# Rest parts of the projection weights on GpSimd instead of VectorE, in a decoder layer on one core

## The reference

```
h = rms_norm(x, attn_norm)
proj = h @ w_in                         # 1024 x 3072: mq mk mv dq dk dv
q, k = rope(rms_norm(q)), rope(rms_norm(k))
moba = softmax(causal(q k^T / 8)) v
diff = rms_norm((softmax(q1 k1^T / 8) - lam * softmax(q2 k2^T / 8)) v) * (1 - lambda_init)
x = x + concat(moba, diff) @ w_out
h = rms_norm(x, ffn_norm)
x = x + (silu(h @ w_gate) * (h @ w_up)) @ w_down      # hidden width 2816
```

## Time and profile before

| | before |
|---|---|
| median of 3 runs | 684.35 us (684.1 to 685.02) |
| profiled execution, span from first to last instruction | 685.7 us |
| TensorE matmul busy | 654.8 us (95%) |
| TensorE weight load busy | 533.4 us (78%) |
| VectorE busy | 366.3 us (53%) |
| ScalarE busy | 247.9 us (36%) |
| GpSimd busy | 79.3 us (12%) |
| chain that ended last, by engine | PE 77%; DVE 14%; issue 4%; ACT 2%; DMA 1% |

### The profile page before, as it was taken

One profiled execution on the slowest core, in us unless ns is written; L12 is line 12 of the kernel. 1 busy time (PEld: TensorE's weight loads), 2 busy tenths in 40 slices (PEclk: granted clock), 3 DMA queues, 4 the chain that ended last, 5 costly groups with the idle time before them and its releaser, 6 DMA issues.

```text
span 685.7 us, 9568 instructions
## 1 busy us (share of the span) xinstructions
PE 654.8 (95%) x3220; PEld 533.4 (78%) x3220; DVE 366.3 (53%) x703; ACT 247.9 (36%) x458; POOL 79.3 (12%) x64
## 2 busy tenths in 40 slices
PE   5989999998898989999999999999999999999998
PEld 5867777786777776879988888888888888888886
DVE  4778788787879788777424242332424242222212
ACT  5354636363554545423422222322222232111110
POOL 0415042240505050000000000000000000000000
PEclk9999999999989898999999999999999999999999
DMA  7303032130404041142232232313232233222103
GB/s 291 109 24 115 16 109 57 66 105 17 124 1 122 0 153 63 40 175 93 65 121 90 94 105 78 122 62 122 71 112 92 92 115 100 93 92 93 62 1 122
DMA packets 19944, 61.42 MB, mean 90 GB/s; under 512 B 3024, under 2 KB 3408, under 8 KB 19920
## 3 DMA queue, kind: packets, MB, share of 16 engines
q1 hardware_dynamic: 19920, 61.11, 26.8%
HBM read 54.80 MB, written 2.10 MB: 83 GB/s over the span
## 4 chain that ended last, share of the span: by engine, by line
PE 77%; DVE 14%; issue 4%; ACT 2%; DMA 1%; SPq 0%; DVEq 0%; ACTq 0%
PE ps L1077 24%; PE ps L1079 23%; PE ps L1078 23%; PE ps L1142 3%; DVE small L713 2%; PE ps L1157 2%; DVE small L716 1%; DVE small L788 1%; DVE small L714 1%; PE ps L1109 1%; DVE w_lo L723 1%; ACT probs L480 1%; DMA w_raw<-wt 1%; DVE probsT_lo L822 1%; PE ps L1117 1%
## 5 line engine op out<-in xcount | busy, mean ns | idle before, releaser
L1077 PE MATMUL ps<-h_parts,w_hi 128*128 128x512 f32 (+1 forms) x576 | 227.5, 395 | 3.0 <-DVE h_parts L859 2.8
L1079 PE MATMUL ps<-h_parts,w_lo 128*128 128x512 f32 (+1 forms) x576 | 220.8, 383 | 0.0
L1078 PE MATMUL ps<-h_parts,w_hi 128*128 128x512 f32 (+1 forms) x576 | 219.0, 380 | 0.0
L723 DVE TENSOR_TENSOR w_lo<-w_raw,w_hi 128x1024 fp32r<-128x1024 f32 x93 | 118.4, 1273 | 79.1 <-ACT w_hi L389 78.8
L1077 PEld LDWEIGHTS ps<-h_parts,w_hi 128*128 128x128 f32 x576 | 109.5, 190 | 26.0 <-issue 7.3
L389 ACT ACTIVATE w_hi<-w_raw 128x1024 fp32r<-128x1024 f32 x93 | 97.4, 1053 | 81.8 <-PE ps L1079 80.4
L1079 PEld LDWEIGHTS ps<-h_parts,w_lo 128*128 128x128 f32 x576 | 109.1, 189 | 22.6
L1078 PEld LDWEIGHTS ps<-h_parts,w_hi 128*128 128x128 f32 x576 | 109.5, 190 | 19.0
L1042 DVE TENSOR_TENSOR gated<-ps,silu_gate 128x512 f32<-128x512 f32 x22 | 15.2, 692 | 154.9 <-PE ps L1079 154.9
L1079 PE MATMUL ps<-w_hi,hidden_parts 128*128 128x512 f32 x176 | 69.3, 394 | 0.0
L1077 PE MATMUL ps<-w_hi,hidden_parts 128*128 128x512 f32 x176 | 69.3, 394 | 0.0
(11 more groups left out here) (141 smaller groups left out, 731.5 us busy)
## 6 DMA issues: line engine op xcount, KB each, us to landing
w_raw<-wt SPq DMA_DIRECT2D x98, 512.0 KB, 3.4
residual<-x SPq DMA_DIRECT2D x4, 512.0 KB, 4.8
q_rotated<-q_gained SPq DMA_DIRECT2D x32, 64.0 KB, 2.0
k_rotated<-k_gained SPq DMA_DIRECT2D x32, 64.0 KB, 2.0
out<-residual SPq DMA_DIRECT2D x8, 256.0 KB, 2.0
ffn_gain<-gain SPq DMA_DIRECT2D x1, 512.0 KB, 3.3
cos<-cos SPq DMA_DIRECT2D x1, 256.0 KB, 7.3
sin<-sin SPq DMA_DIRECT2D x1, 256.0 KB, 7.6
```

What stands on the lines that cost most here:

```text
L723: nc.vector.tensor_tensor(WL[:, slot], RAW[:, slot], WH[:, slot].bitcast(F32), ALU.subtract).then_inc(w_lo, 1)
L1077: nc.tensor.matmul(dst, lh, rh, start=start, stop=False, skip_group_check=True)
L1078: nc.tensor.matmul(dst, lh, rl, start=False, stop=False, skip_group_check=True)
L1079: return nc.tensor.matmul(dst, ll, rh, start=False, stop=stop, skip_group_check=True)
```

## The change

The subtractions for the weight tiles 5 to 25, 21 in all, move from VectorE's list to GpSimd's: `project_lo(p, 2)` ahead of the rope of Q, `project_lo(p, 3)` between the two ropes, `project_lo(p, 4)` between the rope of K and `scale_v`, for p = 1 to 7. Two waits keep the count of `w_lo_ready` in order where one engine takes over from the other: GpSimd waits for 5 ahead of its loop, VectorE for 26 ahead of `project_lo(8, 2)` in period 7. Nothing else changes; TensorE, ScalarE and SyncE keep their lists.

```diff
+            def project_lo(p, j):
+
+                pool.wait_ge(w_hi, p * 3 + (j + 1))
+                nc.gpsimd.tensor_tensor(WL[:, j % 3], RAW[:, j % 3], WH[:, j % 3].bitcast(F32),
+                                        ALU.subtract).then_inc(w_lo, 1)
+
...
             scale_v(0)
+            pool.wait_ge(w_lo, 5)
             with pool.Fori(1, PAIRS) as p:
+                project_lo(p, 2)
                 rope(p, QG, QR, QS, q_ev, q_rot, q_pool, qh_s, ql_s)
+                project_lo(p, 3)
                 rope(p, KG, KR, KS, k_ev, k_rot, k_pool, kh_s, kl_s)
+                project_lo(p, 4)
                 scale_v(p)
...
             with dve.Fori(1, MOBA_PAIRS) as t:
...
                 pt_lo(t, 0, True)
-                project_lo(t + 1, 2)
                 norm(t, 2, True)
                 v_lo(t, True)
                 maxima(t, 3)
-                project_lo(t + 1, 3)
                 pt_lo(t, 1, True)
...
                 k_norm(t + 1)
-                project_lo(t + 1, 4)
                 mix_lo(t, True)
...
             o_sum(6)
             maxima(7, 0)
+            dve.wait_ge(w_lo, G_OUT + 2)
             project_lo(8, 2)
```

More of the change, by code:

```diff
@@ L900, in _ @@
             maxima(0, 2)
-            project_lo(1, 2)
             pt_lo(0, 1, True)
@@ L904, in _ @@
             maxima(0, 3)
-            project_lo(1, 3)
             norm(0, 3, True)
@@ L910, in _ @@
             scales(1)
-            project_lo(1, 4)
             k_norm(1)
@@ L939, in _ @@
             maxima(4, 1)
-            project_lo(5, 2)
             norm(4, 1, False)
@@ L949, in _ @@
             pt_lo(4, 2, False)
-            project_lo(5, 3)
             pt_lo(4, 3, False)
@@ L954, in _ @@
             k_norm(5)
-            project_lo(5, 4)
             with dve.Fori(MOBA_PAIRS + 1, PAIRS - 1) as t:
```

## The result

| | before | after |
|---|---|---|
| median of 4 runs | 684.66 us (684.1 to 685.02) | 721.25 us (716.58 to 722.64) |
| ratio, 95% interval | | 1.0514 [1.0473, 1.0555] |
| span of the profiled execution | 685.7 us | 718.3 us (own time 720.21) |
| mean granted clock over the span | 0.983 | 0.962 |

The forecast was 716 us in a range of 700 to 725. The change costs 5%. The measured 721.25 us lies in that range, but above the 704 to 720 that the prediction gave its own mechanism, and among the 720 to 726 of the rival in which GpSimd keeps the lock.

What follows compares the result with a forecast made beforehand. TensorE was taken as the bound, delayed by the root ahead of K's scale spread. Terms 1.0 + 13.8 + 5.7 + 8.4 + 3 = 31.9 us on the median of 684.35 gave 716 us, range 700 to 725.

Steps and rivals of the forecast that it cites:

- The mechanism: VectorE's reciprocal root stands still while GpSimd computes, one small instruction passing at each GpSimd end; 704 to 720 us, chance 0.68.
- Partial trapping: Rival: each meeting of VectorE and GpSimd costs less than worked out; 696 to 704 us, chance 0.16.
- faster: Rival: VectorE's saved work counts and meetings with GpSimd do not; 680.6 us, chance 0.04.
- no change: Rival: meetings with GpSimd and VectorE's saved work cancel, needing a loss under 1 us a period; chance 0.03.
- GpSimd keeps the lock while it has work: Rival: VectorE stands until GpSimd's list runs out, about 0.6 us more a period; 720 to 726 us, chance 0.09.
- The price of a subtraction: One moved 128x1024 subtraction, 1.22 us on VectorE, was taken to cost 2.5 us on GpSimd.
- The end of a period: Later subtractions delay the root before K's scale spread (line 757): +4.7 us in periods 2 and 4, +4.2 in period 5.
- The early meetings: `project_lo(p, 2)` delays VectorE's line 791 early in a period: 0.8 us in period 2, +1.0 in periods 0 and 4.
- The clock: TensorE's granted clock falls after longer idle times in periods 1 to 6: net +3 us, bounds 0 and +9.
- VectorE's relief: 21 x 1.22 us leave VectorE; TensorE gains 0.7 us a period at exponentials, mostly given back, leaving 0.1 a MoBA period.

Runs made afterwards that it cites:

- the root's layout: Reciprocal root's tiles laid so each small instruction has at most one SBUF operand: changed kernel with it 687.17 us, kernel before with it 672.1 us.
- the kernel with 16 columns: Changed kernel with GpSimd's 21 subtractions cut to 16 of their 1024 columns, the other columns left out: 678.39 us, ratio 0.9891.

## Why the prediction was right

**The mechanism** was the predicted one, at the predicted place, and the root's layout shows it as a cause: without the root's waiting the move costs 15 us instead of 37. *Partial trapping*, *faster* and *no change* fell. *GpSimd keeps the lock while it has work* fell too, though the time of 721.25 us lies among its 720 to 726: when GpSimd's instructions ended at 132.66, 133.90 and 135.30 the turn went to VectorE each time.

**The price of a subtraction** was 2.38 us, where I took 2.5. I had read 2.5 ns a column as a sign that nothing of it was fixed, which one length can't show: by the two lengths measured, 1.28 and 2.38 us, about 0.18 us is fixed. The estimate by the Trainium skill (GPSIMD Engine Reference, section 3.1), 2.35, was nearer.

**The end of a period** was overrated. Line 767, which was 757, came 3.6 us later against Q's rope in period 2, not 4.7: 0.25 for two subtractions, and the 0.7 us by which small VectorE instructions should have pushed GpSimd did not exist; GpSimd's instructions follow each other at 131.37, 132.62, 133.99 and 135.26 as if alone. In the waits that is 4.4 to 4.7 us in a MoBA period instead of 5.6, and 5.9 to 6.2 in periods 4 to 6 instead of 6.8 to 7.7. All waits for the spread came to 31.4 us; I had said about 36.

**The early meetings** were there, and underrated. In period 4 line 801 was held like this:

```profile
182.64 1.69 DVE L801 SCALAR_TENSOR_TENSOR small<-small 128x2 f32<-128x2 f32 x1
```

1.5 us late instead of 1.0, and TensorE stood 1.95 us for the exponentials, after which its clock fell in mid-period (0.50 from 188 to 190 us): the period cost 7.86 us where I had 5.7 without the clock. In period 0 I had seen line 791 but not `project_lo(1, 3)` beside the scaling of the probabilities:

```profile
58.32 0.73 DVE L814 TENSOR_SCALAR probs<-probs,small 128x512 f32<-128x512 f32 x1
58.97 1.48 DVE L815 TENSOR_SCALAR probs<-probs,small 128x512 f32<-128x512 f32 x1
```

(0.49 us each when free; the first is held by the subtraction, the second by the first step of K's rope, late behind it). TensorE waited 1.95 us behind them instead of 0.80, and period 0 cost 3.3 us, not 1.0. With the root out of the way the waits for the exponentials are not longer than without the move (5.3 us against 5.9), so they are no fixed price of these meetings.

**The clock** fell behind each wait, as predicted, but cost about three times the 3 us that I took: TensorE's 9.2 us of additional busy time. A mean granted clock of 0.983 over 685.7 us and of 0.962 over 718.3 us makes some 23 and 55 us at 1.2 GHz, an estimate. The idle times did not swallow the slow stretches as I had assumed; new ones came in the middle of periods 4 and 0.

So the sum of 31.9 us against 32.6 measured in the span is partly luck: the ends of the periods were some 8 us too dear (19.5 us more of waits for the spread, not some 27), the clock 6 and the early meetings 2 to 3 too cheap. Against the medians the sum is 4.7 us short of the 36.6, and only the upper bound of 725, above the 720 that the mechanism was given, holds the result.

**VectorE's relief** was hidden in this; the kernel with 16 columns shows it worth 7 us, where I had counted 0.7 a period at one place only. The prediction put the relief from `project_lo(p, 3)` at nothing, because VectorE then waits anyway. In period 5 of the kernel before it does not: this subtraction runs until the last rest parts ahead of the root, which begin at 216.00:

```profile
214.87 1.21 DVE L723 TENSOR_TENSOR w_lo<-w_raw,w_hi 128x1024 fp32r<-128x1024 f32 x1
```

With 16 columns on GpSimd the waits for the spread in periods 4 to 6 are 0.6 to 0.8 us shorter each (2.33, 2.01 and 2.00 us instead of 2.95, 2.64 and 2.83).

## What to carry to other kernels

Before moving an elementwise step to GpSimd, look at which VectorE instructions run beside it: each with two SBUF inputs (or a scaling from SBUF to SBUF) waits for a GpSimd instruction that reads SBUF to end. A dependent chain of tiny ones was the worst neighbour here, since a link of 0.17 us could lose a whole GpSimd instruction, 1.2 to 2.3 us. VectorE's busy time hides this, because the waiting counts as busy; compare the longest with the median of one form. A chain that can't be moved can be freed, as here, by keeping one input of each link in PSUM. And check the timeline when the time agrees: 716 forecast and 721 measured hid three terms that were off by 2 to 8 us each.

## What was not expected of the hardware

- The small instructions of the root took 0.17 to 0.18 us with an operand in PSUM, as with all of them in SBUF; only the 128x512 copy from PSUM was slower, 0.68 against 0.42 us.
- VectorE's small instructions slipped between GpSimd's without delaying them measurably: in period 2 GpSimd's follow each other as closely (131.37, 132.62, 133.99, 135.26) as if alone.
- The runs of one kernel spread more than the first comparison shows: the kernel before lay within 0.9 us in four runs there, and from 682.2 to 690.78 us in 13 later ones. The changed kernel's four lay within 6 us.
